# Rotary rotations of a second transformer block: where the sine product changes rows

## The reference, cut to what matters

```
half = x.shape[-1] // 2                       # 32 of 64 channels of a head
x1, x2 = xf[..., :half], xf[..., half:]
return concatenate([x1 * cos - x2 * sin, x2 * cos + x1 * sin], axis=-1)

dq, dk = apply_rope(differential attention's queries and keys)   # 4 heads x 2 x 64 channels
nq     = apply_rope(queries of the second attention)             # 8 heads of 64
k_cmp  = compress(apply_rope(kc)),  k_sel = apply_rope(ks),  k_win = apply_rope(kw)
```

## Time and profile before

| | |
|---|---|
| median of 3 runs | 2080.68 us (2080.14 to 2081.94) |
| profiled execution, device time | 2080.7 us |
| its span in the trace | 2078.9 us |
| mean granted TensorE clock | 0.997 |
| PE busy | 2029.1 us (98%) |
| DVE busy | 995.8 us (48%) |
| ACT busy | 904.1 us (43%) |
| POOL busy | 868.2 us (42%) |
| the second block's steps | from about 1262 to about 1575 us of the span |

### The profile page before, as it was taken

How to read it: one execution, slowest core, us unless ns; L and a number is a source line. 1 busy time by engine, 2 the same in 40 slices (tenths; PEclk the granted TensorE clock), 3 DMA queues, 4 the chain that set the end, 5 groups by cost and what they waited for, 6 DMA issues and landing times.

```text
span 2078.9 us, 28471 instructions
## 1 busy us (share of the span) xinstructions
PE 2029.1 (98%) x9900; PEld 1595.8 (77%) x9900; DVE 995.8 (48%) x1563; ACT 904.1 (43%) x1760; POOL 868.2 (42%) x648
## 2 busy tenths in 40 slices
PE   9999999999999999999999999999989999999997
PEld 6777688888887766678888887776667878888886
DVE  6444555312265678662312265666665563223133
ACT  5444543323344664552423356666653343223234
POOL 3222345444454322144444454542113554545454
PEclk9999999999999999999999999999999999999999
DMA  4222123232222111022222222321102223232323
GB/s 151 69 72 81 61 92 101 92 100 94 97 95 97 61 57 45 32 92 95 98 99 93 101 91 81 102 94 49 42 31 73 100 92 100 92 102 93 100 93 109
DMA packets 50581, 177.87 MB, mean 86 GB/s; under 512 B 5537, under 2 KB 5801, under 8 KB 50481
## 3 DMA queue, kind: packets, MB, share of 16 engines
q1 hardware_dynamic: 48096, 172.07, 25.0%
q10 hardware_dynamic: 2384, 4.43, 0.6%
HBM read 174.36 MB, written 2.12 MB: 85 GB/s over the span
## 4 chain that ended last, share of the span: by engine, by line
issue 46%; PE 31%; POOL 19%; DVE 2%; POOLq 1%; ACT 1%; DVEq 0%; ACTq 0%
POOL w_lo L517 19%; PE gemm_banks L542 9%; PE gemm_banks L544 9%; PE gemm_banks L543 9%; PE score_banks L989 1%; PE score_banks L998 1%; PE out_bank L1035 1%; DVE turned L2217 1%; POOLq L511 0%; POOLq L516 0%; ACT tmp L1471 0%; ACT probs L1216 0%; DVE x L2324 0%; PE out_bank L1026 0%; PE gemm_banks L961 0%
## 5 line engine op out<-in xcount | busy, mean ns | idle before, releaser
L517 POOL TENSOR_TENSOR w_lo<-raw,w_hi 128x512 fp32r<-128x512 f32 x644 | 868.0, 1369 | 1193.5 <-ACT w_hi L1106 1193.4
L1106 ACT ACTIVATE w_hi<-raw 128x512 fp32r<-128x512 f32 x644 | 370.9, 623 | 784.9 <-PE gemm_banks L544 777.0
L542 PE MATMUL gemm_banks<-h_hi,w_hi 128*128 128x512 f32 x1512 | 613.1, 406 | 4.4 <-POOL w_lo L517 3.6
L544 PE MATMUL gemm_banks<-h_hi,w_lo 128*128 128x512 f32 x1512 | 590.6, 391 | 0.0
L543 PE MATMUL gemm_banks<-h_lo,w_hi 128*128 128x512 f32 x1512 | 590.3, 390 | 0.0
L542 PEld LDWEIGHTS gemm_banks<-h_hi,w_hi 128*128 128x128 f32 x1512 | 283.1, 187 | 97.8 <-issue 34.6
L542 PE MATMUL gemm_banks<-u_hi,w_hi 128*128 128x512 f32 x864 | 339.3, 393 | 5.6 <-POOL w_lo L517 1.5
L543 PE MATMUL gemm_banks<-u_lo,w_hi 128*128 128x512 f32 x864 | 336.5, 389 | 0.0
L544 PE MATMUL gemm_banks<-u_hi,w_lo 128*128 128x512 f32 x864 | 336.5, 389 | 0.0
L544 PEld LDWEIGHTS gemm_banks<-h_hi,w_lo 128*128 128x128 f32 x1512 | 283.0, 187 | 61.8
L543 PEld LDWEIGHTS gemm_banks<-h_lo,w_hi 128*128 128x128 f32 x1512 | 283.6, 188 | 55.7 <-issue 2.9
(11 more groups left out here) (317 smaller groups left out, 1868.3 us busy)
## 6 DMA issues: line engine op xcount, KB each, us to landing
raw<-slabs SPq DMA_DIRECT2D x322, 512.0 KB, 3.3
table<-rel_rows ACTq DMA_DIRECT2D x4, 512.0 KB, 3.6
x<-x_t SPq DMA_DIRECT2D x4, 256.0 KB, 7.0
x<-x_t ACTq DMA_DIRECT2D x4, 256.0 KB, 7.1
cos<-pos SPq DMA_DIRECT2D x2, 256.0 KB, 10.3
y_t<-x SPq DMA_DIRECT2D x2, 256.0 KB, 2.8
y_t<-x ACTq DMA_DIRECT2D x2, 256.0 KB, 2.7
y_t<-x SPq DMA_DIRECT2D x1, 512.0 KB, 2.8
```

Of the source, the lines that this page charges most:

```text
L517: pool.tensor_tensor(w_lo[:, j, part], raw[:, j, part], w_hi[:, j, part].bitcast(F32), ALU.subtract).then_inc(slab_split, 1)
L542: pe.matmul(out, high, rhs_hi, start=first, stop=False)
L544: return pe.matmul(out, low, rhs_hi, start=False, stop=last)
L1106: act.activation(w_hi[:, m % 2, part], raw[:, m % 2, part], ACT.Copy).then_inc(slab_hi, 1)
```

## The change

The sine product is written straight into the partner's rows. For each group of 32 rows VectorE multiplies the bank's rows `r` to `r+31` by `-scale` and by the same rows of `sin2`, and writes rows `(r^32)` to `(r^32)+31` of `tmp[:, 2 + n % 2]`: four operations of 32 rows in the place of one of 128. ScalarE's function `e_swaps` and its three calls go, and with them 60 copies; the semaphore `swapped` goes with its 15 signals, and so do VectorE's two kinds of wait on it; ScalarE's wait on `rope_ready`, which kept it from overwriting the buffer, goes too. The cosine product, the addition L2108, `gemm_free` behind the cosine product and `rope_ready` stay where they are. `tmp[:, 0]` and `tmp[:, 1]` are no longer used in these rotations.

```
@@ ScalarE @@
-            def e_swaps(h):
-
-                for name, p, turn in ends_of(h):
-                    if name in ROTATED:
-                        n = E_ROPE[name, p]
-                        act.wait_ge(gemm_free, taken_out[name, p])
-                        if n > 2:
-                            act.wait_ge(rope_ready, n - 2)
-                        for r in range(0, P, 32):
-                            o = r ^ 32
-                            last = act.activation(tmp[r:r + 32, 2 + n % 2, :], tmp[o:o + 32, n % 2, :], ACT.Copy)
-                        last.then_inc(swapped, 1)
-
             for h in range(-E_AHEAD, 0):
                 e_half(h)
-                e_swaps(h)
...
-                if s > 0:
-                    e_swaps(2 * s - 1)
-                e_swaps(2 * s)
                 e_half(2 * s + 1)
@@ VectorE, e_second @@
                     n = E_ROPE[name, p]
-                    dve.wait_ge(swapped, n)
                     dst = rotated(name, p)
                     dve.tensor_tensor(dst, dst, tmp[:, 2 + n % 2, :], ALU.add).then_inc(rope_ready, 1)
@@ VectorE, e_first @@
-                if name in ROTATED and E_ROPE[name, p] > 2:
-                    dve.wait_ge(swapped, E_ROPE[name, p] - 2)
                 dve.wait_ge(gemm_full, c.gemm.at(1))
                 c.gemm.now += 1
                 if name in ROTATED:
 
                     scale = QK_SCALE if name in ("q", "nq") else 1.0
-                    dve.scalar_tensor_tensor(tmp[:, E_ROPE[name, p] % 2, :], bank, -scale, sin2[:, :], ALU.mult, ALU.mult)
+
+                    for r in range(0, P, 32):
+                        rows, to = slice(r, r + 32), slice(r ^ 32, (r ^ 32) + 32)
+                        dve.scalar_tensor_tensor(tmp[to, 2 + E_ROPE[name, p] % 2, :], bank[rows, :], -scale,
+                                                 sin2[rows, :], ALU.mult, ALU.mult)
                     last = dve.scalar_tensor_tensor(rotated(name, p), bank, scale, cos2[:, :], ALU.mult, ALU.mult)
```

More of the change, by code:

```diff
@@ L457, in build @@
         rstd_ready, squared_rstd = sem("rstd_ready"), sem("squared_rstd")
-        swapped, rope_ready = sem("swapped"), sem("rope_ready")
+        rope_ready = sem("rope_ready")
         dve_step, act_step = sem("dve_step"), sem("act_step")
```

## The result

The changed kernel is slower. Over five runs it takes 2093.29 us in the median (2088.75 to 2094.87), the kernel before on the same chip 2080.68 us (2080.14 to 2082.92): ratio 1.0055, 95% interval [1.0044, 1.0066]. The direction is the forecast one, but the time lies 5.0 us above the forecast and 1.8 us above the end of the range. The profiled execution is the median one (2093.3 us, span 2091.3, mean granted clock 0.993 where it was 0.997).

A forecast was written before the change was run, and what follows sets the result against it. TensorE was taken as the bound. The columns' 0.3 + 2.1 + 0.9 + 0.4 + 1.2 + 1.3 + 1.4 = 7.6 us on 2080.7 gave 2088.3 us; own case 2086.5 to 2089.8, with rivals 2084.5 to 2091.5.

The forecast's parts named there:

- The first rival: The four products follow each other 0.61 us apart like other VectorE pairs, giving 4.4 us more, 2085.1 us; chance 0.15.
- Start, +0.3: q0, k0, kc ahead of the steps: 4.46 us added to VectorE against 4.36 us of copy waits gone; +0.3 us.
- k1, +2.1: Step 2: only 0.1 us between VectorE's last write and TensorE's use, so +2.1 us.
- k2, +1.6 and -0.7: Step 5: cover 0.6 us, so +1.6; copies leave the path to the split, -0.7; net +0.9 us.
- q3, +0.4: Step 7: cover 1.7 us before TensorE's transposes, so +0.5; taken as +0.4 us (0 to 0.8).
- k3, 0, ks, 0: One of six columns with at least about 2.2 us of cover; taken as 0, up to 0.5 us together.
- nq1, +2.2 and -1.0: Step 18: no cover, +2.2; at step 20 TensorE's 1.0 us wait behind the copies is taken back; net +1.2 us.
- nq2, +1.3: Step 27: 2.23 us added less 0.96 us of VectorE idle time, no copy wait returned; +1.3 us.
- nq3, +2.2 and -0.8: Step 36: TensorE waits for scaling, +2.2; 0.8 returns a step later; net +1.4, up to 0.7 less by a multiplication.
- The long wait at 1530 us: Rival: a small shift ends this wait (2.9 us) and its slow clock (1.7 us), giving 2083.7 us; chance 0.06.
- The clock: Rival: TensorE's clock falls behind nq1's and nq3's waits, at most 1.7 us each; 2090.0 or 2091.7 us; chance 0.23.

The follow-up runs named there:

- one_group: Changed kernel with three sine products per rotation, all from rows 0 to 31 into rows 0 to 31, in place of four that change rows: 2078.08 us, one run.
- split_held: Changed kernel with one more wait: ScalarE's split of half -2 waits until the two additions of q0 and k0 are done: 2089.39 us, ratio 1.0033.
- one_product: Changed kernel with one 128-row sine product in place of four of 32 rows, the exchange of rows left out: 2075.04 us, ratio 0.9965 to the kernel before.
- early_copied: Changed kernel with q0, k0 and kc rotated by ScalarE's copies as before, the other twelve by VectorE's four products: 2088.93 us, ratio 1.0033.
- late_copied: Changed kernel with nq1, nq2 and nq3 rotated by ScalarE's copies as before, the other twelve by VectorE's four products: 2088.05 us, ratio 1.0029.
- nq1_vector: Kernel before with nq1 alone rotated by VectorE's four products: 2083.73 us, ratio 1.0010.
- dma_swaps: Kernel before with ScalarE's four copies of a rotation replaced by four 64 KB DMA transfers issued at the same place: 2091.28 us, ratio 1.0046.

## Why the prediction was right or wrong, by its steps

- **Length and spacing of the products: right.** 2.23 us a rotation was forecast, 3.53 - 1.29 = 2.24 measured. The first rival (0.61 apart) is out, by the 0.70 of all rotations and by one_group's 0.60. (Its "4 x 0.4 = 1.1" does not come out: three columns at 0.4 are 1.2, and its sum would be 4.3.)
- **Start, +0.3: wrong, +3.0.** The step set VectorE's added time against its waits and let everything behind keep its length. It named ScalarE's copies only as a wait that goes; that their going also moves ScalarE's split, and with it GpSimd's subtraction, onto the additions was not followed. split_held shows that the trade itself was right (0.0).
- **k1, +2.1: 1.7 (with step 2, 1.9).** The cover of 0.1 was right. L2064 (L2081 before) takes 1.89 us where it took 2.33 beside GpSimd's subtraction; now it starts when that is over: 0.4 back. TensorE's wait before L1026 is 1.43 us, where 2.0 was forecast.
- **k2, +1.6 and -0.7: +1.1 and -0.8.** The wait of L1026 is 1.36 us (forecast 1.5). The missing 0.5 is an older wait for `w_lo` (1321.4 us, 0.3 us long by its row), behind q2's copies, that goes: one_product has it as -0.6.
- **q3, +0.4: -0.1.** Its cover of 1.7 us was read right. The rotation starts 0.4 us earlier against TensorE than before, and the combination behind it takes 0.75 us where it took 1.10, so what is added stays inside the cover.
- **k3, 0: -0.8. Left out.** TensorE waited 0.55 us for `w_lo` behind k3's copies, at 1362.37. "Four such places" should have been seven, with q2's, k3's and kc's (0.86 us at 1289.4); the list of waits above has four at L542 for `w_lo`, 2.0 us, beside the one at L905 that I followed, and I had followed none of the four.
- **ks, 0: +0.7. Wrong.** The cover of "at least about 2.2 us" held with the lengths of before. Here the combination (L2220, at 1381.84) lasts 1.83 us (0.75 before), beside the subtraction that starts at 1380.60, and TensorE waits for it. In one_product, with the shift of 2.2 us absent, it does not happen.
- **nq1, +2.2 and -1.0: +3.2 and -1.1, of it 1.5 by the clock.** The wait grew by 2.3, as forecast, but "scores and scaling of step 19 keep that distance" was wrong: 0.7 comes back at step 21, as one_group shows. **nq2, +1.3: +1.2, right. nq3, +2.2 and -0.8: +1.6 and -0.9 in early_copied**: the multiplication of 0.89 us has become 0.16, the bound that I had named and not taken; TensorE's wait is 1.98 us, not 2.6. In after the two rows are 1.4 us more, by the clock.
- **The long wait at 1530 us**: it stays, as forecast.
- **The clock: wrong, 6.7 us in the traced execution.** It was a rival with a chance of 0.23 and at most two falls of 1.7 us. There are four more slow stretches than before, and the old one has double length. The sentence "nothing shows what one of 2.6 us does" was not true, since it looked at this stage alone: the same trace, in the first block, has a wait of 2.70 us, and half speed behind it.

```profile
796.82 1.54 PE L843 MATMUL score_banks<-consts,probs 128*128 128x128 f32 x6 [2.70 <-ACT probs L1369]
```

```profile
796.00:800.00 4.00, 3.18 (x13) 2.89 (x14) 3.85 (x11) 2.27 (x7) 0.10 (x1) 0.57 0.03 12
```

With it and the wait of 3.3 us, both followed by half speed, the fall should have been the likelier case. The new waits of 1.4 us in steps 2 and 5 did leave the clock alone. v0's wait of 3.5 us, longer than the 3.3 us at 1530, was not foreseen at all, since it came from the wrong term of the start, and neither was a stretch behind a wait as short as the 1.37 us at 1583.

Without the clock the columns add to 5.9 us, against my 7.6. This is nearer than it deserves, since misses cancel: +1.6 at the start with step 2 and +0.7 at ks against -0.8 at k3, -0.8 at k2 and step 4, -0.7 at nq3, -0.6 at nq1, -0.5 at q3 and -0.5 at k1 and nq2. So the mechanism behind the direction was right, the sum without the clock is in part luck, and what put the time outside the range is the clock, with the start's missed collision, which brought one of its stretches.

**What stays open.** At 1583 us the clock falls in after, and in split_held and late_copied, but not in before, though TensorE had done nearly the same ahead of it. Busy times before (1568 to 1576 us) and then after:

```profile
1568.00:1572.00 4.00, 2.25 (x28) 1.78 (x30) 1.77 (x2) 2.36 (x4) 2.09 (x2) 1.00 0.02 4
1572.00:1576.00 4.00, 4.00 (x30) 3.30 (x29) 1.35 (x2) 2.51 (x3) 0.40 (x1) 1.00 0.41 131
```

```profile
1579.00:1583.00 4.00, 2.24 (x28) 1.76 (x26) 1.60 (x2) 2.18 (x4) 2.26 (x2) 0.98 0.02 4
```

2.25 against 2.24 us busy of 4, and half speed follows once only. The profile does not show what decides, and none of the runs tells it. It is 1.6 of the 12.6 us. The same is seen where all twelve kernels are still alike, in the first block: the wait at 797 us, 2.70 to 2.74 us long, is followed by half speed in ten traces and not in split_held and late_copied, one of 1.32 us at 878 us in two (nq1_vector and one_group). Split_held at the first place:

```profile
796.00:800.00 4.00, 3.19 (x17) 2.44 (x17) 3.86 (x10) 2.16 (x7) 0.55 (x1) 1.00 0.01 2
```

So one and the same wait brings the slow clock in one execution and not in another, and a price of the clock read from single traces, as here, is that of one execution. The Trainium skill ("TensorE: Matmul & The Clock Gate", section "Part 1: The HAM clock gate (the 'warmup' mystery)") says that the activity is judged in windows that run freely and don't start with the kernel. That would let the same work fall differently, as it does here at 797 us; no run shows that this is the reason. The prices of the single slow stretches at the start and at nq1 are what the waits leave of a row, worked out above and not measured by themselves.

## What to carry to other kernels

Work that leaves an engine moves everything queued behind it, also towards other engines: follow it two releases on, here ScalarE's split and then GpSimd's subtraction, and ask beside which of VectorE's operations with two SBUF inputs that now falls. An exchange of rows costs VectorE by the operation, not by the row, so four of 32 rows are worth it only where the timeline shows more than the added 2.2 us between the engine's last write and TensorE's use of it, or where the other engine's copies are themselves waited for; decided column by column, with some copies and splits moved as well, it gave -5.9 us in the place of +12.6. And where a change gives TensorE a long wait, count the slow clock behind it as a likely part of its price: in the second block's steps every wait of 2.35 us or more was followed by it in all twelve traces, one of 1.98 us in two of the four that have it (after and dma_swaps, not early_copied and split_held).

## What the runs showed of the hardware

- An operation of VectorE on 32 rows out of PSUM, 512 columns fp32, lasts 0.686 us, as on 128 rows. The next one starts 0.60 us after it in the same rows, 0.70 us where the rows change (one_group and after).
- An addition of 128x512 fp32 with both inputs in SBUF takes 0.69 us alone and up to 1.75 us beside GpSimd's subtraction, the combination 0.75 and 1.83 us. Products with one input in PSUM don't change (0.70 us apart in both).
- Issuing a transfer of 64 KB inside SBUF takes ScalarE's queue 0.63 us, as long as copying the 32 rows itself, and the data land 2.0 us after the issue in the median of the first 16, 2.2 us over all 60 (dma_swaps).
- A wait of TensorE of 2.70 us is followed by 3.4 us at 1.2 GHz in one kernel (after, nq1) and 6.8 us in another (nq1_vector), and by none in two of twelve traces of the same wait (797 us).
